# Last stage of a hybrid decoder step: two token tiles mixed from early gathers and from results still on chip

## What is computed

```python
    _, idx = lax.top_k(jnp.where(in_group, sel, -jnp.inf), TOP_K)      # TOP_K = 2 of 16 experts
    wts = jnp.take_along_axis(scores, idx, axis=-1)
    wts = wts / jnp.sum(wts, axis=-1, keepdims=True)
    ...
    act = jax.nn.silu(hg) * hu * combine[..., None].astype(t.dtype)
    out = jnp.einsum('tef,efd->td', act, w_down)
    ...
        x = x + gt2 * grouped_moe(hn, w_router, b_router, w_gate, w_up, w_down)
    ...
    y = rms_norm(x, final_g)
```

## Time and profile before

| what | value |
|---|---|
| median of 3 runs | 1131.13 us (1132.61, 1131.13, 1127.16) |
| the profiled execution's own time | 1127.33 us |
| its span, first to last instruction | 1125.6 us |
| busy: PE, DVE, ACT, POOL | 1023.6, 575.9, 355.0, 225.3 us |
| mean granted TensorE clock | 0.944 |
| slots: first gate product to end of last down product | about 833 to 1065 us of the span |
| end of last down product to the end | 1065 to 1125.6 us |

### The profile page before, as it was taken

How to read it: one execution, slowest core, us unless ns; L and a number is a source line. 1 busy time by engine, 2 the same in 40 slices (tenths; PEclk the granted TensorE clock), 3 DMA queues, 4 the chain that set the end, 5 groups by cost and what they waited for, 6 DMA issues and landing times. The chain is left out here.

```text
span 1125.6 us, 15469 instructions
## 1 busy us (share of the span) xinstructions
PE 1023.6 (91%) x5432; PEld 603.1 (54%) x5432; DVE 575.9 (51%) x1272; ACT 355.0 (32%) x729; POOL 225.3 (20%) x366
## 2 busy tenths in 40 slices
PE   3899999899999889978998989999769999999975
PEld 3466666544587677766887445444433333333332
DVE  3243445777435856568883253547672332332248
ACT  6121221114311364332331443333213333332333
POOL 0100000068341334413111000002142121111060
PEclk9999999999999888897997999999869999999988
DMA  9685525201011510038761920131447977699283
GB/s 333 201 236 190 217 85 214 75 39 76 38 15 29 117 38 1 1 92 280 268 227 30 339 75 20 41 129 38 134 121 254 333 246 253 231 354 366 106 321 132
DMA packets 126930, 177.07 MB, mean 157 GB/s; under 512 B 37406, under 2 KB 81683, under 8 KB 126840
## 3 DMA queue, kind: packets, MB, share of 16 engines
q1 hardware_dynamic: 117510, 147.03, 38.8%
q0 software_dynamic: 6432, 18.96, 5.1%
q10 hardware_dynamic: 2906, 10.02, 2.2%
HBM read 129.06 MB, written 45.85 MB: 155 GB/s over the span
## 5 line engine op out<-in xcount | busy, mean ns | idle before, releaser
L371 PE MATMUL bank<-hw 128*128 128x344 f32 x576 | 169.7, 456 | 3.8 <-ACT hw L555 3.8
L371 PEld LDWEIGHTS bank<-hw 128*128 128x128 f32 x576 | 109.8, 191 | 62.0 <-issue 5.4
L2232 PE MATMUL bank<-hw,H 128*64 (+1 forms) x608 | 135.1, 597 | 2.1 <-ACT hw L2312 2.1
L456 PE MATMUL bank<-hw 128*128 128x512 f32 x256 | 114.7, 605 | 4.3 <-ACT qkvT L583 4.3
L2668 PE MATMUL bank<-hw 128*128 128x512 f32 x232 | 106.5, 602 | 0.5 <-DVE hw L1974 0.5
L2232 PEld LDWEIGHTS bank<-hw,H 128*64 128x64 f32 x608 | 44.0, 138 | 88.9 <-issue 88.9
L456 PEld LDWEIGHTS bank<-hw 128*128 128x128 f32 x256 | 64.2, 254 | 50.5 <-issue 32.1
L2250 PE MATMUL bank<-yy,H 128*64 128x512 f32 (+1 forms) x304 | 71.1, 611 | 2.2 <-ACT H L2291 2.1
L2312 ACT ACTIVATE hw<-hw 128x2048 f32 x19 | 36.3, 1911 | 109.1 <-PE bank L2232 90.2
L2335 DVE COPY H<-bank 128x256 f32<-128x256 f32 x19 | 8.1, 424 | 115.6 <-PE bank L2215 115.6
L2668 PEld LDWEIGHTS bank<-hw 128*128 128x128 f32 x232 | 41.7, 190 | 44.1 <-issue 41.5
(11 more groups left out here) (565 smaller groups left out, 1833.5 us busy)
## 6 DMA issues: line engine op xcount, KB each, us to landing
ys_d<-ZO SPq DMA_DIRECT2D x18, 1024.0 KB, 12.9
yy<-in_w_down SPq DMA_DIRECT2D x16, 1024.0 KB, 10.4
hw<-in_w_gate SPq DMA_DIRECT2D x16, 1024.0 KB, 7.3
hw<-in_w_up SPq DMA_DIRECT2D x16, 1024.0 KB, 10.9
ys_d<-H ACTq DMA_DIRECT2D x19, 512.0 KB, 6.9
hw<-in_w_in SPq DMA_DIRECT2D x4, 2048.0 KB, 8.2
yy<-in_w_ada SPq DMA_DIRECT2D x4, 2048.0 KB, 8.7
hw<-in_w_ada SPq DMA_DIRECT2D x8, 1024.0 KB, 12.2
```

Of the source, the lines that this page charges most:

```text
L371: mm = t.matmul(ps[3 * (m % 2) + s][:, 0:SEG], w_ring[:, q % 2, k, (m % 4) * P:(m % 4 + 1) * P], hT[:, k, s * SEG:(s + 1) * SEG], start=(k ...
L456: mm = t.matmul(ps[b % 4][0:n, :], tok, w_ring[:, q % 2, k, :], start=(k == 0), stop=(k == KD - 1))
L2232: mm = t.matmul(ps[2 + p][lane, :], xT[p][:, k, lane], wgu[:, bass.ds(bufs[j], 1), k, :].rearrange("p o n -> p (o n)"), start=(k == 0), st ...
```

## The change

Every result row of the last two slots is still on chip in `yo` when the last down products are done. The change lets the token tiles 0 and 1 use that, and gathers the rest of their rows earlier.

- DVE, at the end of `body(1)`, runs `split_rows`: from the row numbers and shares it works out which rows of tiles 0 and 1 lie in the last two slots (near) and which before them (far). It writes far row numbers (a row of zeros in place of a near one), far shares, and 0/share matrices `near` for the two slots.
- PE, at the end of `body(3)`, transposes the four `near` matrices into bank 7; ACT copies them to `share` and makes four diagonals `diag_far`.
- POOL, in its tail, waits for the stores of all but the last two slots and issues eight indirect DMAs of 256 KB for the far rows (half rows, into a free gate/up weight buffer), four per token tile.
- PE, behind the last down products, mixes tile 0 (four far products, four near ones) into banks 0 and 1 and tile 1 likewise into banks 2 and 3.
- The wait for all stores and the signal `y_done` move from ACT to DVE. POOL then gathers tiles 2 to 8 only, tiles 2 and 3 once the first far mix is done, the others once the second is.
- The prompt's gt2 products and their copies move ahead to the router, behind the last logits; the sample tokens' move behind the mix of tile 3.

```diff
+        near = [scan_room[:, 0:512].rearrange("p (i m n) -> p i m n", i=2, m=2),
+                chosen_room[:, 0:512].rearrange("p (i m n) -> p i m n", i=2, m=2)]
+        share = chosen_room[:, 0:512].rearrange("p (i m n) -> p i m n", i=2, m=2)
+        diag_far = counted_room[:, 0:512].rearrange("p (i j n) -> p i j n", i=2, j=2)
+        bound = scan_room[:, 512:513]
+        at_near = [scan_room[:, 516 + 4 * m:520 + 4 * m].rearrange("p (j i) -> p j i", j=2) for m in range(2)]
+        is_far, far_f = (scan_room[:, 524 + 4 * m:528 + 4 * m].rearrange("p (j i) -> p j i", j=2) for m in range(2))
+        scale_far = scan_room[:, 532:536].rearrange("p (i j) -> p i j", i=2)
...
+        pos_far = scan_room[:, 536:544].bitcast(U32).rearrange("p (h i j) -> p h i j", h=2, i=2)
+        far_pair = scan_room[:, 544:552].rearrange("p (h i j) -> p h i j", h=2, i=2)
+        ys_halves = ys_d.rearrange("r (h n) -> (r h) n", h=2)
...
+        far_in, far_mixed, mixed = [sem(f"far_in{n}") for n in range(2)], sem("far_mixed"), sem("mixed")
...
+        ya_far = [[[wgu[:, 1, 4 * i + 2 * j + half_, :] for half_ in range(2)] for j in range(2)] for i in range(2)]
...
             def tail(s):
                 weights(s, dn_in, 5, 16, dn_ready)
+                g.wait_ge(gu_ps, s)
+                for n in range(2):
+                    g.wait_ge(y_out[(s - n) % 2], 16 * ((s - n) // 2))
+                fdve.wait(g, "far")
+                for i in range(2):
+                    for j in range(2):
+                        for half_ in range(2):
+                            g.indirect_dma_start(ya_far[i][j][half_], None, ys_halves, bass.IndirectOffsetOnAxis(ap=pos_far[:, half_, i, j:j + 1], axis=0)).then_inc(far_in[i], 16)
                 g.wait_ge(x_in[(s + 1) % 2], 16 * ((s + 1) // 2 + 1))
...
+                if s == 3:
+                    fdve.wait(t, "near")
+                    for i in range(2):
+                        for m in range(2):
+                            mm = t.transpose(ps[7][:, (2 * i + m) * P:(2 * i + m + 1) * P], near[0][:, i, m, :], ident[:, :])
+                    fpe.did(mm, "share")
+
+            def mix_far(i):
+                t.wait_ge(far_in[i], 64)
+                for half_ in range(2):
+                    for j in range(2):
+                        mm = t.matmul(ps[2 * i + half_][:, :], diag_far[:, i, j, :], ya_far[i][j][half_], start=(j == 0), stop=False, skip_group_check=True)
+                mm.then_inc(far_mixed, 1)
+
+            def mix_near(i, m, y, last):
+                for half_ in range(2):
+                    mm = t.matmul(ps[2 * i + half_][:, :], share[:, i, m, :], y[:, half_ * 512:(half_ + 1) * 512], start=False, stop=last, skip_group_check=True)
+                return mm
 
             def tail(s):
                 act_transposes(s)
                 down(s, buffers(s))
+                t.wait_ge(xT_sb, s + 2)
+                fact.wait(t, "diag_far")
+                mix_far(0)
+                t.wait_ge(y_half, s)
+                t.wait_ge(y_sb, s)
+                mix_near(0, 0, yo[(s - 1) % 2], False)
+                t.wait_ge(y_half, s + 1)
+                t.wait_ge(y_sb, s + 1)
+                mix_near(0, 1, yo[s % 2], True).then_inc(mixed, 1)
+                mix_far(1)
+                mix_near(1, 0, yo[(s - 1) % 2], False)
+                mix_near(1, 1, yo[s % 2], True).then_inc(mixed, 1)
...
-            def tail(s):
-                out(s)
-                for p in range(2):
-                    a.wait_ge(y_out[p], 16 * ((s + 2 - p) // 2))
-                a.activation(sg[0][:, 0:1], sg[0][:, 0:1], ACT.Copy).then_inc(y_done, 1)
+                if s == 3:
+                    fpe.wait(a, "share")
+                    fact.did(a.activation(share.rearrange("p i m n -> p (i m n)"), ps[7][:, :], ACT.Copy), "share")
+                    for i in range(2):
+                        for j in range(2):
+                            fact.did(a.activation(diag_far[:, i, j, :], ident[:, :], ACT.Copy, scale=scale_far[:, i, j:j + 1]), "diag_far")
...
-            tiles(a, body, tail)
+            tiles(a, body, out)
...
-            tiles(v, body, a_copy)
+                if s == 1:
+                    split_rows()
+
+            def split_rows():
+
+                f = lambda ins, name=None: (fdve.did(ins, name), fdve.drain(v))
+                dve.wait(v, "combine")
+                f(v.tensor_scalar(bound, ex[:, 1, EXPERTS - 1:EXPERTS], 1.0 / LANES, 0.5 - 0.5 / LANES, ALU.mult, ALU.add))
+                f(v.tensor_scalar(bound, bound, ROUND, -ROUND, ALU.add, ALU.add))
+                f(v.tensor_scalar(bound, bound, float(P), -2.0 * P, ALU.mult, ALU.add))
+                f(v.tensor_scalar(at_near[0], col[:, 5:7, 0:2], bound, None, ALU.subtract))
+                f(v.tensor_scalar(at_near[1], at_near[0], -float(P), None, ALU.add))
+                f(v.tensor_scalar(is_far, at_near[0], 0.0, None, ALU.is_lt))
+                f(v.tensor_tensor(scale_far.rearrange("p i j -> p j i"), combine[:, 0:2, :].rearrange("p i j -> p j i"), is_far, ALU.mult))
+                f(v.tensor_scalar(far_f, col[:, 5:7, 0:2], -NO_ROW, None, ALU.add))
+                f(v.tensor_tensor(far_f, far_f, is_far, ALU.mult))
+                f(v.tensor_scalar(far_f, far_f, NO_ROW, None, ALU.add))
+                for half_ in range(2):
+                    f(v.tensor_scalar(far_pair[:, half_].rearrange("p i j -> p j i"), far_f, 2.0, float(half_), ALU.mult, ALU.add))
+                f(v.tensor_copy(pos_far, far_pair), "far")
+                for j in range(2):
+                    for i in range(2):
+                        for m in range(2):
+                            fdve.did(v.tensor_scalar(near[j][:, i, m, :], pos_n[:, :], at_near[m][:, j, i:i + 1], combine[:, i, j:j + 1], ALU.is_equal, ALU.mult))
+                fdve.drain(v)
+                fdve.did(v.tensor_tensor(near[0], near[0], near[1], ALU.add), "near")
+            def tail(s):
+                a_copy(s)
+                for p in range(2):
+                    v.wait_ge(y_out[p], 16 * ((s + 2 - p) // 2))
+                v.tensor_copy(bound, bound).then_inc(y_done, 1)
+            tiles(v, body, tail)
...
         def fin_gpsimd(g):
             dve.wait(g, "pos")
             g.wait_ge(y_done, 1)
-            for i in range(9):
-                n = P if i < NT else DEC
-                if i >= YA:
+            for i in range(2, 9):
+                n, b = P if i < NT else DEC, (i - 2) % YA
+                g.wait_ge(far_mixed, 1 if i < 4 else 2)
+                if i >= YA + 2:
                     fpe.wait(g, f"mix{i - YA}")
                 for j in range(2):
-                    g.indirect_dma_start(ya[i % YA][0:n, j, :], None, ys_d, bass.IndirectOffsetOnAxis(ap=pos[0:n, i, j:j + 1], axis=0)).then_inc(ygot[i % YA], 16)
+                    g.indirect_dma_start(ya[b][0:n, j, :], None, ys_d, bass.IndirectOffsetOnAxis(ap=pos[0:n, i, j:j + 1], axis=0)).then_inc(ygot[b], 16)
 
         def fin_tensor(t):
-            for half_ in range(2):
-                for k in range(4):
-                    t.matmul(ps[2 + half_][:, k * P:(k + 1) * P], modT[:, GT2 + 4 * half_ + k, 0:1].to_broadcast([P, P]), ident[:, :], start=True, stop=True)
-                    mm = t.matmul(ps[(7, 4)[half_]][0:DEC, k * P:(k + 1) * P], modT[:, GT2 + 4 * half_ + k, 1:9], ident[:, :], start=True, stop=True)
-            fpe.did(mm, "gt2")
-            for i in range(9):
-                n = P if i < NT else DEC
+            for i in range(2, 9):
+                n, b = P if i < NT else DEC, (i - 2) % YA
                 fact.wait(t, f"diag{i}")
-                if i == 1:
-                    fact.wait(t, "gt2")
-                t.wait_ge(ygot[i % YA], 32 * (i // YA + 1))
-                if i >= 2:
+                t.wait_ge(ygot[b], 32 * ((i - 2) // YA + 1))
+                if i >= 3:
                     fdve.wait(t, f"g{i - 2}")
                 for half_ in range(2):
                     for j in range(2):
-                        mm = t.matmul(ps[(5, 2)[i % 2] + half_][:, :], diag[0:n, i % 2, j, :], ya[i % YA][0:n, j, half_ * 512:(half_ + 1) * 512],
+                        mm = t.matmul(ps[(5, 2)[i % 2] + half_][:, :], diag[0:n, i % 2, j, :], ya[b][0:n, j, half_ * 512:(half_ + 1) * 512],
                                       start=(j == 0), stop=(j == 1))
                 fpe.did(mm, f"mix{i}")
+                if i == 3:
+                    for half_ in range(2):
+                        for k in range(4):
+                            mm = t.matmul(ps[(7, 4)[half_]][0:DEC, k * P:(k + 1) * P], modT[:, GT2 + 4 * half_ + k, 1:9], ident[:, :], start=True, stop=True)
+                    fpe.did(mm, "gt2")
...
-            diagonals(0)
-            diagonals(1)
-            fpe.wait(a, "gt2")
-            for half_ in range(2):
-                c = slice(half_ * 512, (half_ + 1) * 512)
-                fact.did(a.activation(gt2P[:, c], ps[2 + half_][:, :], ACT.Copy))
```

(46 more changed lines are left out.)

## The result

The changed kernel takes **1123.95 us** (median of ten runs, 1119.41 to 1125.56); the kernel before, beside it, 1129.47 us (1127.16 to 1133.17). The measured ratio is 0.994, 95% interval 0.9923 to 0.9957, which is 6.8 us less (the two medians differ by 5.5 us, the two means by 6.4). Two later series give 0.9936 (0.9915 to 0.9957) and 0.9925 (0.9898 to 0.9952). The forecast was 1123.5, from 1118 to 1130.5. The profiled execution after took 1122.33 us, span 1120.6, against 1127.33 and 1125.6 before.

A forecast was written before the change was run, and what follows sets the result against it. PE was taken as busiest, with DVE's 4 us beat bounding the last stage from tile 4. 7.0 - 0.44 - 0.6 = 6.0 us gave 1121.3 against the profiled execution; adding 2.2 us to the mean gave 1123.5, range 1118 to 1130.5.

The forecast's parts named there:

- The tail: Last stage on PE: 56 records and eight gt2 products without DMA waits start tile 4's "g" 7.0 us earlier.
- The beat behind it: Last stage from tile 4 on: DVE's own work keeps an unchanged beat of 4 us per tile.
- The price of a gt2 product: On PE: 0.32 us each for sample tokens; for the prompt 0.42 at full clock, 0.84 at half.
- The router: Prompt's gt2 ahead of the counting products delays the ranks: 0.6 us more, bounds 0 and 1.2.
- Slot 3: Four added transposes on PE in body(3), where PE has no idle time: 0.44 us more.
- Added DVE and ACT work: In the slots: split_rows' 5.2 to 7.0 us fit DVE's 7.36 us wait, ACT's copies its idle time: nothing.
- The sum: Whole kernel: 7.0 - 0.44 - 0.6 = 6.0 us less, 1121.3 us against the profiled execution.
- The first: Rival at the last down products: the clock does not fall, PE starts 1.7 us earlier, 1121.8 us; chance 0.13.
- The second: Rival in the last stage: POOL's gathers land late, PE waits, 1124.5 to 1126.6 us; chance 0.2.
- the covers: Time by which far gathers land before PE needs them: 2 us for tile 0, 4 for tile 1.
- The third: Rival in the tail: half clock stays for PE's records, the kernel is slower, near 1149 us; chance 0.08.

The follow-up runs named there:

- e2: The changed kernel with each far product done twice, 16 more records of 512 columns on PE: 1131.72 us, ratio 0.9994 to the kernel before.
- e5: The changed kernel with the prompt's gt2 products moved behind the router's last counting products: 1122.58 us, ratio 0.9928 to the kernel before.
- e4: The changed kernel with slot 3's near transposes and the sample tokens' gt2 moved into PE's gap ahead of the last down products: 1121.58 us, ratio 0.9908.
- after_again: The changed kernel run a second time, nothing altered: 1124.55 us, ratio 0.9936 to the kernel before.
- after_third: The changed kernel run a third time, nothing altered: 1125.36 us, ratio 0.9925 to the kernel before.
- e3: The changed kernel with the far gathers waiting for the stores of all slots: 1140.36 us, ratio 1.0072 to the kernel before.
- e6: The changed kernel with the moves of e5 and e4 together: 1122.08 us, ratio 0.9908 to the kernel before.
- e1: The kernel before with only the prompt's gt2 products and their copies moved to the router: 1131.46 us against 1131.93, ratio 0.9984.

## Why the prediction was right, step by step

- **The tail, 7.0 us; measured 7.43.** PE's line of 56 records and the gt2 products sets tile 4's "g", as the chain, e2, and the 26.31 to 26.32 us in the three traces of the changed kernel and in e5 show. Two sizes were off and partly cancel: the sixteen records of gt2 took 1.84 us, not 2.5; the 56 others 24.48 with the short steps between their groups, not 24.1 and 0.1.
- **The beat behind it, taken as unchanged; it was.** The prediction says that DVE's own work sets the 4 us. The chain shows a round of 8.11 us for two tiles over DVE, ACT and PE, as in e4's lines above: 1094.17 to 1102.28 after, 1099.12 to 1107.23 before. DVE's own work is within 0.2 us of it, so the reading cost nothing here; that a quicker DVE alone would change the beat does not follow from these rows.
- **The price of a gt2 product.** I read it from the start of one L2439 to the start of L2440, where products of two forms alternate. In an unbroken row of one form a product of the sample tokens takes 0.23 us at full clock (1.84 over 8), not 0.32, and one of the prompt 0.47 at half clock (3.76 over 8), not 0.84. A whole row of the prompt's at full clock is in no trace. The router's term rested on the same price.
- **The router, 0.6 us taken of 0 to 1.2; measured 0.** The ranks wait for DVE at either clock. The rows show the clock rising with these products in seven of the ten traces that have them in the router, and not in after_again, after_third and e5. The rule of the Trainium skill, page "TensorE: Matmul & The Clock Gate", section "What's actually happening", that activity releases the clock, agrees with the seven and not with the three, in one of which PE was busy without a break from 811.8 to 818.0 and stayed at 0.50. The result that the prediction drew from the rule, a term of 0, held in all ten, because the products are cheap enough at half clock too.
- **Slot 3, 0.44 us; measured 0.73.** The slots' distance from one set of down products to the next is 11.70 us, and 12.43 in slot 3. Half of a row of eight transposes left out what a small group costs by itself: the four take 0.59 us to the next gate product, and the rest of the 0.73 us lies at the ends of the products around them:

```profile
880.17 3.65 PE L2272 MATMUL bank<-yy,H 128*64 x16
883.75 0.66 PE L2290 MATMUL bank<-ident,small_room 128*128 128x128 f32 x4
884.34 7.09 PE L2254 MATMUL bank<-hw,H 128*64 x32
...
892.60 0.65 PE L2272 MATMUL bank<-yy,H 128*64 x2
```

(PE's timeline of the changed kernel; the last row is cut off by the end of the window that was asked for.)

- **Added DVE and ACT work, nothing; measured nothing.** DVE's split_rows took 5.5 us, from 860.27 to 865.78, and DVE then still waited 1.92 us for PE at L2387, where it had waited 7.36.
- **The sum.** 7.43 - 0.73 = 6.7 us from the traces, for 6.0 forecast; the three series give 6.8, 7.2 and 8.5 us (ratio by the median of before beside it). The three errors, gt2 in the tail, gt2 in the router, transposes, are each below 0.7 us, and the transposes' works against the other two. That the median came out within 0.5 us of the forecast is in part luck: ten runs of the changed kernel spread over 6 us. The prediction's bound for "faster", 1125.5, was taken from a median of 1131.13; against the 1129.47 measured beside the change it would be 1123.8, and the change stands just above that, so it is the interval of the ratio that shows it faster.
- **The rivals.** The first, a clock that doesn't fall in the last down products, came true in the profiled execution, at its price of 1.7 us, but as scatter of either kernel. The second had its long issue, and the covers, 2.3 and 4.3 us against 2 and 4 forecast, held. The Trainium skill, page "SBUF — State Buffer", section "SBUF: two separate sides", by which some DVE operations hold up POOL's descriptors, spoke for it; the trace has the long issue, but no run shows what made it long, and nobody waited for a gather. The third did not come: the tail runs at full clock throughout (granted clock 1.00 from 1067.8 to 1094.0), and e3 shows half clock coming back behind a pause of 12.43 us.

## What to carry to other kernels

Where a stage opens with a store, a gather and a landing in a row, look for operands that exist earlier or are still on chip; the gain is what the new line of work ends earlier at the point where the old bound takes over again (here the fifth tile), not the length of the waits removed. Price small products from an unbroken row of the same form, and small groups between large ones with their seams. Before a difference between two traces is put down to the change, take each kernel's trace once more.

## What the runs showed of the hardware

- An idle time of about 2.1 us ahead of the last down products was followed by half clock in five of nine traces of closely related kernels and not in four, with no relation to its length (2.06 to 2.22 us where it fell, 2.06 to 2.21 where it did not).
- The sixteen gt2 records of 128 columns were followed by a rise of the clock in seven traces, 2.8 to 3.4 us after their start in six (e6: 4.4, behind their end), and by none in three. During the 36 small records ahead of the gate products, with PE busy throughout, the clock stayed at 0.50 in ten traces, had just fallen to it in e6, and rose in them in after_third (835.5), where they took 2.55 us instead of 3.2.
- The last store on the old path took 2.6 us in both traces of before and 4.89 in e1; the changed kernel's line from the last down products to tile 4 takes 26.31 to 26.32 us in all three of its traces, since no DMA is in it any more.
